# Differential attention units: the distance term moves to VectorE, the key turns and the sigmoids move forward

## The reference

```
z = einsum(q, k) * HEAD_DIM ** -0.5
z = z - slopes[h] * (q_pos - k_pos)          # distance term; NEG_INF where k_pos > q_pos
p = softmax(z)                               # for each of the two components
a = p[:, 0] - lam * p[:, 1]
out = einsum(a, v)
```

## Time and profile before

| | us |
|---|---|
| median of 3 runs | 1315.53 (1315.05 to 1315.6) |
| the profiled execution, its own time | 1318.82 |
| its span in the trace | 1316.9 |
| stage of the differential units, rounds 8 to 15 | 186.40 to 275.24 in the span |
| first piece on the chain of the expert stage | 350.29 in the span |

### The profile page before, as it was taken

How to read it: one execution, slowest core, us unless ns; L and a number is a source line. 1 busy time by engine, 2 the same in 40 slices (tenths; PEclk the granted TensorE clock), 3 DMA queues, 4 the chain that set the end, 5 groups by cost and what they waited for, 6 DMA issues and landing times.

```text
span 1316.9 us, 19565 instructions
## 1 busy us (share of the span) xinstructions
PE 1269.1 (96%) x7690; PEld 515.0 (39%) x7691; DVE 457.0 (35%) x983; ACT 261.5 (20%) x606; POOL 85.3 (6%) x92
## 2 busy tenths in 40 slices
PE   7999999999999999999999999999999999999995
PEld 6355446654433333333333333333333333333331
DVE  0265457866723322223322222332222332222225
ACT  1243348742511101001101000110100110100002
POOL 2023235300020000000000000000000000000000
PEclk9999999999899999999999999999999999999998
DMA  9669889993699999999999995999999999999992
GB/s 353 256 250 373 313 316 381 368 375 113 259 367 407 428 429 426 429 428 429 429 427 428 428 429 232 406 426 429 430 427 429 427 428 429 428 428 427 428 429 87
DMA packets 53308, 498.38 MB, mean 378 GB/s; under 512 B 6793, under 2 KB 7945, under 8 KB 26386
## 3 DMA queue, kind: packets, MB, share of 16 engines
q1 hardware_dynamic: 41746, 430.68, 78.3%
q0 software_dynamic: 11520, 67.11, 13.1%
HBM read 493.58 MB, written 3.93 MB: 378 GB/s over the span
## 4 chain that ended last, share of the span: by engine, by line
PE 47%; DMA 23%; ACT 2%; issue 1%; DVE 0%; SPq 0%; ACTq 0%; DVEq 0%
PE psum L2096 25%; DMA arena<-in_w_gate_up 23%; PE psum L2143 11%; PE psum L1462 4%; PE psum L2077 3%; PE psum L1477 2%; PE psum L1470 1%; ACT arena L2173 1%; ACT arena L2192 1%; DVE arena L2338 0%; PE psum L2044 0%; PE psum L2063 0%; DVE arena L2313 0%; ACT L2209 0%; ACT arena L2203 0%
## 5 line engine op out<-in xcount | busy, mean ns | idle before, releaser
L2096 PE MATMUL psum<-arena 128*64 128x512 f32 x2112 | 462.2, 593 | 11.8 <-DMA arena<-in_w_gate_up 11.2
L2096 PEld LDWEIGHTS psum<-arena 128*64 128x64 f32 x2112 | 150.9, 137 | 316.0 <-issue 287.7
L2143 PE MATMUL psum<-arena 128*64 128x512 f32 x1056 | 233.9, 595 | 3.3
L2281 DVE TENSOR_SCALAR arena<-psum 128x512 f32<-128x512 f32 x33 | 22.8, 692 | 613.2 <-PE psum L2096 613.2
L2143 PEld LDWEIGHTS psum<-arena 128*64 128x64 f32 x1056 | 72.9, 137 | 150.2 <-issue 131.9
L2234 DVE SCALAR_TENSOR_TENSOR arena<-psum,arena 128x1024 f32<-128x1024 f32 (+1 forms) x96 | 103.3, 1103 | 69.4 <-PE psum L2081 37.2
L2188 ACT ACTIVATE arena<-arena 128x512 f32<-128x512 f32 x33 | 20.8, 630 | 455.6 <-DVE arena L2281 455.6
L1462 PE MATMUL psum<-arena 128*64 128x512 f32 x408 | 93.4, 592 | 0.0
L1192 DVE STREAM_TRANSPOSE arena<-arena 128x1024 f32<-128x1024 f32 x64 | 75.2, 1218 | 2.2 <-DVE arena L1292 1.1
L2077 PE MATMUL psum<-arena 64*128 64x512 f32 x264 | 65.9, 615 | 2.3 <-issue 2.3
L2196 ACT ACTIVATE arena<-psum 128x512 f32<-128x512 f32 x33 | 19.7, 597 | 239.8 <-PE psum L2143 239.8
(11 more groups left out here) (265 smaller groups left out, 1006.0 us busy)
## 6 DMA issues: line engine op xcount, KB each, us to landing
arena<-in_w_gate_up SPq DMA_DIRECT2D x128, 2048.0 KB, 19.5
arena<-in_w_down SPq DMA_DIRECT2D x62, 2048.0 KB, 16.5
arena<-in_w_in SPq DMA_DIRECT2D x12, 1024.0 KB, 11.5
arena<-in_w_out SPq DMA_DIRECT2D x4, 1024.0 KB, 10.5
arena<-in_w_down SPq DMA_DIRECT2D x4, 1024.0 KB, 8.5
arena<-in_x_prompt SPq DMA_DIRECT2D x4, 512.0 KB, 4.8
out<-arena SPq DMA_DIRECT2D x8, 256.0 KB, 5.5
arena<-in_ln_g SPq DMA_DIRECT2D x2, 512.0 KB, 7.2
```

The lines of the kernel that those rows point to most:

```text
L2096: ins = nc.tensor.matmul(psum[64 * h:64 * h + 64, n, :], x_k, slot[k][:, col:col + 512], start=False, stop=(k == KD - 1))
L2143: ins = nc.tensor.matmul(psum[64 * h:64 * h + 64, 7, :], h_k, slot[s][:, col:col + 512], start=(k == 0), stop=(k == KD - 1))
```

## The change

Three edits, in the differential rounds alone, and an order of two signals.

1. The distance term is no longer a matmul. `maxima(u)` begins with a VectorE `tensor_tensor` that reads the scores from PSUM, adds `const["abias"]` and writes the sum to SBUF (`leaning`: the buffers `keep` and `left`, which the stick units have done with). The maximum and the exponentials read the sum. The bank is released (`z_used`) by VectorE after the addition.
2. VectorE's round is `turn_keys(u+1, 0)`, `store_rows(u-2)`, `maxima(u)`, `turn_keys(u+1, 1)`, `distances_of_piece(p)` where there is one, `factors(u-1)`, and then the piece.
3. ScalarE's round has `keep_piece(p)` ahead of `exponents(u)`.

```
@@ score_unit
-                    if y:
-                        nc.tensor.matmul(z_of(u, h), ident, const["abias"], start=True, stop=False)
                     pe.wait_ge(keys_turned, 2 * u + h + 1)
...
-                                                   start=(y == 0 and d == 0), stop=(d == 1))
+                                                   start=(d == 0), stop=(d == 1))
@@ sigmoids
+                        act.sem_inc(z_used, 1)
                         act.sem_inc(kept, 1)
-                        act.sem_inc(z_used, 1)
@@ exponents
+                        z = leaning[u % 2][:, h, :]
-                        own.mark(nc.scalar.activation(past_keys(W[u % 2][:, h, :]), past_scores(u, h), ACT.Exp,
+                        own.mark(nc.scalar.activation(past_keys(W[u % 2][:, h, :]),
+                                                      z[:, 0:QUARTER].rearrange("p (s c) -> p c s", s=RUN), ACT.Exp,
...
                     own.wait()
                     act.sem_inc(w_ready, 1)
-                    act.sem_inc(z_used, 1)
@@ ScalarE, round u
-                    exponents(u)
                     if PIECES[p][0] == 0:
                         keep_piece(p)
+                    exponents(u)
@@ maxima
                     dve.wait_ge(scored, 2 * u + 2)
-                    own.link(nc.vector.tensor_reduce(row_max[:, 0:2], psum[:, 2 * (u % 2):2 * (u % 2) + 2, 0:KEYS_Q], AX.X, ALU.max))
+                    z, distance = leaning[u % 2], const["abias"].rearrange("p (o k) -> p o k", o=1).to_broadcast([P, 2, KEYS_Q])
+                    own.link(nc.vector.tensor_tensor(z, psum[:, 2 * (u % 2):2 * (u % 2) + 2, 0:KEYS_Q], distance, ALU.add))
+                    dve.sem_inc(z_used, 1)
+                    own.link(nc.vector.tensor_reduce(row_max[:, 0:2], z, AX.X, ALU.max))
@@ VectorE, round u
-                    maxima(u)
-                    store_rows(u - 2)
                     if more:
                         turn_keys(u + 1, 0)
+                    store_rows(u - 2)
+                    maxima(u)
+                    if more:
+                        turn_keys(u + 1, 1)
                     if PIECES[p][0]:
                         distances_of_piece(p)
                     if p:
                         factors(u - 1)
-                    if more:
-                        turn_keys(u + 1, 1)
```

More of the change, by code:

```diff
@@ L316, in decoder_step @@
         lam_in, lam_tmp = w_past[0][:, 0:4 * HD], w_past[1][:, 0:4 * HD]
+        leaning = [keep, left[:, :, 0:KEYS_Q]]
         Z = [psum[:, 0:2, :].rearrange("p b c -> p (b c)"), psum[:, 2:4, :].rearrange("p b c -> p (b c)")]
@@ L990, in exponents @@
                     for h in range(2):
-                        own.mark(nc.scalar.activation(past_keys(W[u % 2][:, h, :]), past_scores(u, h), ACT.Exp,
+                        z = leaning[u % 2][:, h, :]
+                        own.mark(nc.scalar.activation(past_keys(W[u % 2][:, h, :]),
+                                                      z[:, 0:QUARTER].rearrange("p (s c) -> p c s", s=RUN), ACT.Exp,
                                                       bias=minus_max[u % 2][:, h:h + 1], accum_out=row_sum[:, h:h + 1]))
-                        own.mark(nc.scalar.activation(W[u % 2][:, h, QUARTER:KEYS_Q], z_of(u, h)[:, QUARTER:KEYS_Q], ACT.Exp,
+                        own.mark(nc.scalar.activation(W[u % 2][:, h, QUARTER:KEYS_Q], z[:, QUARTER:KEYS_Q], ACT.Exp,
                                                       bias=minus_max[u % 2][:, h:h + 1], accum_out=own_sum[:, h:h + 1]))
```

## The result

| | before | after |
|---|---|---|
| median, same chip | 1315.6 (5 runs, 1315.05 to 1317.16) | 1329.6 (5 runs, 1323.96 to 1329.78) |
| ratio, 95% interval | | 1.009, 1.0074 to 1.0105 |
| span of the profiled execution | 1316.9 | 1327.9 |

The change makes the kernel 0.9% slower. The time forecast was 1317.9, the range 1313.5 to 1320.5; the time is outside it, on the side that the prediction had at 0.43.

What follows compares the result with a forecast made beforehand. Bound: TensorE and the experts' weight loads; in attention, an 11.12 us VectorE-TensorE round. Terms -2.9 + 0.1 + 1.4 + 0.2 + 1.6 + 0.3, plus 0.4 and clock 1.45, give +2.55; 2.4 taken on 1315.53: 1317.9, range 1313.5 to 1320.5.

Steps and rivals of the forecast that it cites:

- one fall: Rounds 14 and 15: TensorE's longer waits bring the granted clock down once, costing 1.45 us.
- its own ring: Rounds 10 to 13: ScalarE's sigmoids, exponentials and table loads with TensorE's mixing close a chain of waits of 11.50 us.
- The two matmuls removed: TensorE's distance-term matmuls: taking them out gains nothing, as they run during the wait for key turns.
- Rival (b): Clock stays down across rounds 14 and 15, or falls in round 8 too: 1320 us, chance 0.22.
- 0.06 more: A unit's exponentials on ScalarE, read from SBUF: 0.06 us above 1.52, bounds -0.15 and +0.15.
- Round 8: First key turn moves into VectorE's idle time: turn_weights at 193.4 instead of 196.32, gain 2.9 us.
- Round 14's rest for `factors`: TensorE idle 3.8 us before the scores, which wait for factors behind the distances; round still 1.2 early.
- Round 15's exponentials: They follow maxima now behind store_rows(13), so turn_weights comes at 272.2, 0.4 us late.
- The shift: A shift of the attention stage passes one to one into the expert stage, which starts at 350.29 us.
- a drain on top: ScalarE's table loads: a drain of about 1380 ns per switch, from the Trainium skill, left out of the forecast.
- rival (c): ScalarE's chain does not close, rounds fall to about 10.8 us: 1312.8 us, chance 0.10.
- the terms of round 9: VectorE's line of store_rows, maxima, turn, factors, then scores and TensorE's 3.86: 11.26 us against 11.2.

Runs made afterwards that it cites:

- e9: The kernel after, unaltered, run and profiled once more as anchor: 1.0083 against the kernel before.
- e10: The kernel after with unread matmuls in TensorE's waits for weights and for the last unit's second score: 1.0027 against the kernel before.
- e1: The kernel before with only ScalarE's new order, the piece's sigmoids ahead of the unit's exponentials: 1.001.
- e16: The kernel before with VectorE's new order in round 8 alone and unit 8's distances added by VectorE in place in PSUM: 1.0012.
- e2: The kernel before with only VectorE's new order, key turns around store_rows and maxima: 1.0003.
- e7: The kernel after with ScalarE's old order, exponentials ahead of the sigmoids: 1.0039 against the kernel before.
- e5: The kernel after with the sum written back to PSUM and read there by the exponentials: 1.005 against the kernel before.
- e14: The kernel before, unaltered, run and profiled again: 1.0008.
- e8: The kernel before with both new orders, VectorE's and ScalarE's, the distance term still on TensorE: 1.0032.
- e13: The kernel after with the sum in place in PSUM, factors ahead of the second key turn, and shorter unread matmuls in TensorE's waits: 1.0009 against the kernel before.
- e15: The kernel before with VectorE's new order in round 8 alone, distances still on TensorE: 1.0.

## Why the prediction was wrong

**The clock (the step that failed).** "I count one fall, +1.45". The trace after has the clock down in rounds 10, 11, 14, 15 and behind them. What that cost is 8.3 us by this trace (2.2 in rounds 10 and 11, 6.1 behind round 13, worked out below), 10.0 between the profiled runs of e9 and e10, and 0.0056 of the time, 7.4 us, between all their runs. The step looked for long rests only, those of rounds 14 and 15. The rests of about 1 us that its own ring makes in each of the rounds 10 to 13 it did not count, and one rest of 1.47 that left the clock at 1.00 spoke for leaving them out. But that was one rest among rounds with almost none; after the change every round has two. One cause stands in the prediction as worth nothing: "The two matmuls removed are worth nothing: TensorE does them while it waits for the key turns". They cost no time where they stood, but in round 12 TensorE is busy for 9.97 us instead of 10.91 without them, and e10, with two unread matmuls of their size in each round, keeps its clock. And the price of a fall, 1.45, was read from round 8; where the low clock covers a whole round, as in round 11, TensorE itself becomes the bound (busy 13.07 of 13.34). Rival (b) was this mechanism with a chance of 0.22 and the same small price, 1320.

The Trainium skill's rule that waits between bursts bring the clock down ("TensorE: Matmul & The Clock Gate", section "HAM oscillation — how this bites in real kernels") was cited for one fall. The trace after agrees with it for the clock of 0.88 in round 14, where TensorE waits 3.10 us. That the clock is down in rounds 10 and 11 as well (0.91 and 0.71), after waits of 0.82 and 1.04 us in round 10, is more than the forecast drew from it.

**The exponentials from SBUF (the second step).** "I take 0.06 more, bounds a tenth either way". They take 0.53 more per unit (2 x 0.264), some nine times that and outside the bounds. In the ring it shows whole: 12.02 to 12.03 in rounds 12 and 13 against 11.5, and 12.24 in rounds 10 and 11 of e9 against 11.7. No row of before had a strided read from SBUF; the bounds should then have come from what a stride could cost, not from a tenth.

**What held.** Round 8: `turn_weights` 7.08 us after the round's start, forecast 7.0 (193.4 - 186.40). The addition 0.708, forecast 0.71. The ring through `keep_piece`, `exponents`, `mix_piece` and `store_piece` binds, with the waits where they were said to be; e1 shows it alone. Only VectorE's wait for `turn_rows`, forecast at about 1 us, is 2.06 at the end of round 12. With the exponentials at their measured price the lengths of rounds 10 to 13 are off by 0.05 at most. Round 14's rest for `factors` 3.10, forecast 3.8. Round 15's exponentials wait for maxima behind `store_rows`. The shift passes into the expert stage one to one. The table loads are 1.28 us with the activation 0.02 behind (236.80 to 238.10), so a drain on top was rightly left out.

**What was overlooked.** The stage begins 2.8 us earlier after the change. 0.64 of it is round 7, which has two matmuls fewer and takes 10.15 us instead of 10.79; the runs of e16, which has the same, win nothing. The other 2.15 arise ahead of round 7, where the two kernels differ only in the order of two signals: the kernel before starts that round at 175.61, and e1 and e2, which have that part unaltered, at 172.89 and 174.40. So that part can be no more than the difference between two profiled runs.

Two sums of the prediction are off by a little: five rounds of 10.8 us gain 2.1, not the 2.3 of rival (c), and the terms of round 9 add up to 11.21, not 11.26. Round 9 took 11.49 at full clock.

**The sum again.** -2.8 (start) - 2.8 (round 8) + 6.1 (rounds 9 to 13: 1.5 forecast, 2.1 exponentials, 2.2 clock by 13.33 and 13.34 against 12.24 in e9, 0.3 left over) + 9.3 behind them (2.1 forecast, about 1.0 exponentials, about 6.1 clock) = +9.8. The term of rounds 14, 15 and the tail without the clock is in e10: 13.58 + 9.10 + 9.65 = 32.33 us against 38.44 after.

## What to carry to other kernels

An operand that moves from PSUM to SBUF keeps its access pattern but not its price: look at the stride, and give it bounds of its own when it lies in a ring. Before an edit that makes a loop's ring wait on another engine, count TensorE's rests per round, not the longest one; in this kernel rests that repeat cost the clock over several rounds, and that was dearer than the rests. For the same reason work that hides in a wait is not always worth nothing: taking it away lengthens the rest. A loss of that kind is measured by filling the rests with unread matmuls no longer than they are, and one profiled run does not decide it, since the stretches of low clock differ from run to run.

## What the runs showed of the hardware

ScalarE's exponential of 128x256 float32 with an inner step of 32 elements: 474 ns from PSUM, 738 from SBUF, 501 from SBUF with unit stride. VectorE's addition: 708 ns into SBUF, 717 in place in PSUM (528 elements each), and 1085 for 512 elements when it writes SBUF with an inner step of 8 elements.

The granted clock fell to 0.50 in a train of rounds with two rests of TensorE in each, 0.8 to 1.1 us long, and stayed at 1.00 in the same rounds with one of the two filled (e9, e10). It did not fall in the same round each time: rounds 10 and 11 in the trace after, rounds 12 and 13 in e9. Nor does the length of the rests decide it alone: e7 kept 1.00 through rounds 10 to 13 with a rest ahead of the scores, 1.05 to 1.21 us, in each of rounds 11 to 13, and e5 lost it in rounds 12 and 13 behind rests of about 0.5.

On the chips where the kernel before takes 1334 to 1336 us, round 9 takes 22 us in it (e14), twice its length elsewhere:

```profile
203.52:225.64 22.12, 16.77 (x143) 8.24 (x143) 9.11 (x19) 8.65 (x22) 10.36 (x11) 0.77 0.92 358
```

The other kernels of these chips show it too (21.0 to 22.8 us, e5 to e8, e13, e15, e16). In that round `mix_values` goes through its matmuls almost one by one between 209 and 217 us in e14, with 0.3 to 1.8 us between them; what they wait for was not looked into.
